# Two row units of the first token pass's down projection are added to the residual by one VectorE instruction

## Chip, cores and metric

The kernel runs on one core of a Trainium2 chip. The metric is the device time of one execution in microseconds (us), as the median of several runs. Engines are named as in the profile: PE is TensorE's matmul side, PEld its weight loads, DVE is VectorE, ACT is ScalarE, POOL is GpSimd, SP is the engine that issues most DMAs.

## The reference

The program is one step of a streaming encoder layer on 1152 tokens (1024 of a prompt, 8 x 16 of samples), with D = 1024 and a feed-forward width of 2816. After a convolution branch and an attention branch it computes:

```
def block_output(x, y_conv, y_attn, g_conv, g_attn, w_out, norm_ffn_w, w_gate, w_up, w_down):
    merged = jax.nn.sigmoid(g_conv) * y_conv + jax.nn.sigmoid(g_attn) * y_attn
    x = x + merged @ w_out
    xn = rms_norm(x, norm_ffn_w)
    return x + (jax.nn.silu(xn @ w_gate) * (xn @ w_up)) @ w_down
```

The change lies in the last line, in the sum of x and the product with w_down.

## The kernel before

All matrix products are done in fp32 accuracy with three passes of fp32r operands: high part by high part, low by high, high by low. So each weight block is split into a high part (by ACT, line 949) and a low part (by POOL, line 675). The split blocks go through a ring of 8 slots in SBUF.

The feed-forward part runs in two token passes. The first pass (p = 0) has token tiles 0, 2, 1, 3 of 128 tokens, the second (p = 1) has tiles 4, 6, 5, 7, 8. Within a pass the width 2816 is cut into 11 chunks of 256. For each chunk PE computes:

- a pair for w_gate (m = 0) and a pair for w_up (m = 1), each as seven products of a Strassen-Winograd scheme (line 1790, 12 matmuls each, into banks 0 to 3). DVE and ACT take the products out of PSUM as they come: ACT copies the first out as `prod` (line 1006), DVE makes the sums `u2`, `u3` and the gates (lines 1380 to 1417);
- then the down projection of the chunk before (function `down`, line 1851): for each half hf of the 1024 output columns, one row unit for each token tile. A row unit is six matmuls of 128x512 into one PSUM bank. In the first pass a down projection has 8 row units, numbered 0 to 7 in what follows (4 tiles for hf = 0, then 4 for hf = 1).

Row units of the down projection go round four banks, 4 to 7. PE may begin row unit n only when row unit n - 4 has been added to the residual X, because they share a bank:

```
if n >= 4:
    pe.wait_ge(y_free, n - 3)
```

`y_ready` counts row units that PE has finished, `y_free` those that DVE has added. `add_row` (line 1437) does one such addition, of 128x512 in PSUM to 128x512 of X in SBUF.

DVE works in program order. In chunk c, behind the pair for w_up, its order is: four `weight_sums` instructions (lines 1322 to 1327, sums of raw weight blocks for a later pair), the additions of row units 0 and 1, `h_lo_part` (line 1423, the low part of this chunk's activations, which waits for ACT), the additions of row units 2 to 7, four more `weight_sums`, and then line 1380 of the next pair. ACT's split of a summed block waits for the `weight_sums` instruction that makes it, and `prod` of the next pair stands behind such a split in ACT's order. PE's fifth product of a pair waits for `prod`, its sixth for the DVE's line 1390.

The last two chunks of the first pass are joined (the border, `border_down`) and keep their own order.

Of the kernel before, what the change touches and what calls it, by code (L numbers as in the profile page):

```python
# [28 lines left out]
ALU = mybir.AluOpType  # L29
# [50 lines left out]
PASS_TILES = ((0, 2, 1, 3), (4, 6, 5, 7, 8))  # L80
# [15 lines left out]
LAST_POS = {ht: n for n, ht in enumerate(LAST_ROWS)}  # L96
LAST_BASE = 6 * NT
# [3 lines left out]
def pair_unit(p, c, m):  # L101

    return 33 * p + (m if c == 0 else 3 * c - 1 + m)


def down_unit(p, c):

    return 33 * p + (4 + 3 * c if c < NCH - 1 else 32)
# [14 lines left out]
SLOT0, PROD0, ROW0 = [0], [0], [0]  # L123
# [9 lines left out]
def row_bank(n):  # L133

    return n % 4 + (0 if BORDER[0] <= n < BORDER[1] else 4)
# [25 lines left out]
def build(nc, io):  # L161
    ctx = ExitStack()
    with ctx:
# [3 lines left out]
        def sem(name):  # L167
            return ctx.enter_context(nc.semaphore(name))
# [87 lines left out]
        banks = ctx.enter_context(nc.psum_tensor("banks", [P, 8, 512], F32))  # L256
# [31 lines left out]
        d_ready, d_free = sem("d_ready"), sem("d_free")  # L288
# [7 lines left out]
        y_ready, y_free, border_used = sem("y_ready"), sem("y_free"), sem("border_used")  # L296
# [769 lines left out]
        def _(dve):  # L1066
# [5 lines left out]
            def norm_scale(ph, t):  # L1072

                xn, wbc = ((xn_p, wbc_p), (xn_f, wbc_f))[ph]
                pos = NORM_POS[t] if ph else t
                q = NT * ph + pos
                dve.wait_ge(sd_done, q + 1)
                dve.reciprocal(rms[:, t:t + 1], sd[:, t:t + 1]).then_inc(rms_done, 1)
                if ph == 0 and t >= 2:
                    dve.wait_ge(nT_done, 2 * (t - 1))  # L1080
                if ph == 1 and pos >= 2:
                    dve.wait_ge(tr_done, 2 * (pos - 1))
                dve.wait_ge(rms_done, q + 1)
                dve.scalar_tensor_tensor(out=xn[:, pos % 2, :], in0=X[:, t, :], scalar=rms[:, t:t + 1], in1=wbc[:, :],
                                         op0=ALU.mult, op1=ALU.mult).then_inc(xn_ready, 1)
# [227 lines left out]
            def weight_sums(r):  # L1313

                p, c, m = UNIT[r]
                q = pair_no(p, c, m)
                dve.wait_ge(f_raw[r % 2], 16 * RAW_PIECES * (r // 2 + 1))
                if r >= 3:
                    dve.wait_ge(f_lo, SLOT0[pair_unit(*divmod(q - 2, PAIRS)[:1], (q - 2) % PAIRS // 2, q % 2) + 1])
                elif r == 0:  # L1320
                    dve.wait_ge(d_ready, LAST_BASE)
                dve.tensor_tensor(w_sum(q, 0), raw_block(r, 1, 0), raw_block(r, 1, 1), ALU.add).then_inc(f_sum, 1)
                dve.wait_ge(f_sum, 4 * q + 1)
                dve.tensor_tensor(w_sum(q, 1), w_sum(q, 0), raw_block(r, 0, 0), ALU.subtract).then_inc(f_sum, 1)  # L1324
                dve.tensor_tensor(raw_block(r, 1, 0), raw_block(r, 0, 0), raw_block(r, 1, 0), ALU.subtract).then_inc(f_sum, 1)
                dve.wait_ge(f_sum, 4 * q + 2)
                dve.tensor_tensor(w_sum(q, 2), raw_block(r, 0, 1), w_sum(q, 1), ALU.subtract).then_inc(f_sum, 1)  # L1327

            def mix(i):

                def step(x, a, b):
                    dve.tensor_tensor(mix_cols(xc_f, i, x), a, b, ALU.subtract).then_inc(xc_T, 1)  # L1332

                dve.wait_ge(xc_copy, 3 * i + COPY_POS[B11])
                step(T1, mix_block(i, "B12"), mix_cols(xc_f, i, B11))
                dve.wait_ge(xc_copy, 3 * i + COPY_POS[B21 if i == 2 else B22])
                dve.wait_ge(xc_T, 4 * i + T_POS[T1])
                step(T2, mix_block(i, "B22"), mix_cols(xc_f, i, T1))
                dve.wait_ge(xc_copy, 3 * i + COPY_POS[B21])
                dve.wait_ge(xc_T, 4 * i + T_POS[T2])  # L1340
                step(T4, mix_block(i, "B21"), mix_cols(xc_f, i, T2))
                step(T3, mix_cols(xc_f, i, B22), mix_block(i, "B12"))

            def mix_lo(i, x):

                dve.wait_ge(xc_hi, 7 * i + HI_POS[x])
                dve.wait_ge(xc_T, 4 * i + 4)
                dve.tensor_tensor(mix_cols(xc[1], i, x), mix_cols(xc_f, i, x), mix_cols(xc[0], i, x).bitcast(F32),
                                  ALU.subtract).then_inc(xc_lo_dve, 1)

            def last_add(n):
                hf, t = LAST_ROWS[n]
                x = X[:, t, hf * 512:(hf + 1) * 512]
                dve.wait_ge(d_ready, LAST_BASE + n + 1)
                dve.wait_ge(d_free, NT * (4 + hf) + t + 1)
                dve.tensor_tensor(x, banks[:, 4 + n % 4, :], x, ALU.add).then_inc(d_free, 1)
# [62 lines left out]
            def h_lo_part(p, c):  # L1419
                ci, nb = NCH * p + c, HALF[p]  # L1420
                dve.wait_ge(h_hi, ci + 1)
                h = h_act[ci % 2]
                dve.tensor_tensor(h[:, 1, :, 0:2 * nb], Gt[ci % 2][:, :, 0:2 * nb], h[:, 0, :, 0:2 * nb].bitcast(F32),
                                  ALU.subtract).then_inc(h_lo, 1)

            def add_row(p, c, hf, k):
                tiles = PASS_TILES[p]
                t = tiles[k]
                n = ROW0[down_unit(p, c)] + len(tiles) * hf + k
                x = X[:, t, hf * 512:(hf + 1) * 512]  # L1430
                dve.wait_ge(y_ready, n + 1)
                if c == 0:
                    dve.wait_ge(d_free, LAST_BASE + LAST_POS[hf, t] + 1)
                else:
                    before = c - (2 if (p, c) == (0, NCH - 1) else 1)
                    dve.wait_ge(y_free, ROW0[down_unit(p, before)] + len(tiles) * hf + k + 1)
                dve.tensor_tensor(x, banks[:, row_bank(n), :], x, ALU.add).then_inc(y_free, 1)  # L1437

            def sums_ahead(r):
                if r + 2 < UNITS and UNIT[r + 2][2] < 2:  # L1440
                    weight_sums(r + 2)

            for p in range(2):
                last = NCH - 1
                for c in range(NCH):
                    border = p == 0 and c == last
                    pair(p, c, 0)
                    if (p, c) == (0, 0):
                        for n in range(14, len(LAST_ROWS)):
                            last_add(n)  # L1450
                    sums_ahead(pair_unit(p, c, 0))
                    if p == 0 and c in SCALE_AT:
                        norm_scale(1, SCALE_AT[c])
                    if p == 0 and c - TAIL_CHUNK in (1, 2):
                        for x in ((T2, T3), (T1, T4))[c - TAIL_CHUNK - 1]:
                            mix_lo(2, x)
                    if c == 1:
                        h_lo_part(p, 0)
                    pair(p, c, 1)
                    sums_ahead(pair_unit(p, c, 1))  # L1460
                    if border:
                        h_lo_part(p, c)
                        sums_ahead(down_unit(p, c - 1))
                        mix(3)
                        norm_scale(1, 7)
                        for k in range(len(PASS_TILES[p])):
                            add_row(p, c, 0, k)
                        for x in (T1, T4):
                            mix_lo(3, x)
                        mix(4)  # L1470
                        for k, x in enumerate((T2, T3, T1, T4)):
                            mix_lo(4, x)
                            add_row(p, c, 1, k)
                    elif c:
                        for hf in range(2):
                            for k in range(len(PASS_TILES[p])):
                                add_row(p, c - 1, hf, k)
                                if hf == 0 and k == 1:
                                    h_lo_part(p, c)
                        sums_ahead(down_unit(p, c - 1))  # L1480
                if p == 1:
                    for hf in range(2):
                        for k in range(len(PASS_TILES[p])):
                            add_row(p, last, hf, k)
                sums_ahead(down_unit(p, last))
# [435 lines left out]
```

## Time and profile before

| | |
|---|---|
| Median of 3 runs | 1702.14 us (1701.66 to 1703.0) |
| Profiled execution | 1702.15 us |
| Span of the profiled execution | 1700.4 us |
| PE busy | 1673.7 us (98%) |
| DVE busy | 959.4 us (56%) |
| POOL busy | 886.6 us (52%) |
| ACT busy | 694.9 us (41%) |

The span is the time from the first to the last instruction, and 1.75 us lie around it. Busy time of PE comes from matmuls whose ends are modelled, so the places where PE lost time are read from the starts of weight loads and from the lengths of the pieces in the chain that ended last.

### The profile page before, as it was taken

To read this page: it belongs to the slowest core of one execution; us is meant where nothing else is said; L and a number is where in the kernel's file an instruction comes from. 1 tells how busy PE (TensorE), PEld (TensorE's weight loads), DVE (VectorE), ACT (ScalarE), POOL (GpSimd) and SP (SyncE) were. 2 spreads that over 40 slices of the span, in tenths; PEclk is the share of its full clock that TensorE was granted. 3 is DMA by queue.
4 is the path that set the end of the run, shared out by engine and by line. 5 is a ranking of instruction groups with operands and counts; after the bars stand their busy time and mean duration, and the time that the engine had idled before them with its cause. 6 is when DMAs were issued, how large, how long until landed. Compare 5 with 4: busy or idle time off the path is not lost.

```text
span 1700.4 us, 27837 instructions
## 1 busy us (share of the span) xinstructions
PE 1673.7 (98%) x10510; PEld 1567.6 (92%) x10510; DVE 959.4 (56%) x1520; ACT 694.9 (41%) x1567; POOL 886.6 (52%) x808
## 2 busy tenths in 40 slices
PE   7999999999999999999999999999999999999999
PEld 7999888899889999999888899999989999999998
DVE  5466665636563412322568666757777555655555
ACT  6333566636665111111116444454454333333331
POOL 3544443333431212121239887887889656666662
PEclk9999999999999999999999999999999999999999
DMA  5211111111110111114121333233233222222222
GB/s 176 47 38 37 47 33 35 41 30 46 33 32 26 50 38 38 50 37 161 39 87 38 100 99 112 88 101 112 100 118 106 92 83 74 76 86 80 83 87 74
DMA packets 136057, 120.29 MB, mean 71 GB/s; under 512 B 24195, under 2 KB 117663, under 8 KB 135937
## 3 DMA queue, kind: packets, MB, share of 16 engines
q1 hardware_dynamic: 130400, 115.89, 21.7%
q10 hardware_dynamic: 4896, 2.36, 0.5%
q8 instruction: 76, 1.25, 0.3%
q0 software_dynamic: 640, 0.43, 0.1%
q14 instruction: 45, 0.36, 0.1%
HBM read 113.33 MB, written 5.32 MB: 70 GB/s over the span
## 4 chain that ended last, share of the span: by engine, by line
PE 94%; DVE 3%; issue 1%; ACT 1%; DMA 0%; SPq 0%; POOL 0%; DVEq 0%; ACTq 0%
PE banks L1504 37%; PE banks L1790 28%; PE banks L1851 15%; PE banks L1729 5%; PE banks L1667 2%; PE banks L1649 2%; PE banks L1527 1%; PE banks L1629 1%; PE banks L1540 1%; PE banks L1638 0%; DMA X<-in_x_prompt 0%; DVE w_sums L1327 0%; DVE xc_full L1332 0%; DVE w_sums L1324 0%; PE banks L1672 0%
## 5 line engine op out<-in xcount | busy, mean ns | idle before, releaser
L1504 PE MATMUL banks<-x_hi,w_hi 128*128 128x384 f32 x1200 | 410.7, 342 | 0.0
L1504 PE MATMUL banks<-x_hi,w_lo 128*128 128x384 f32 x1200 | 401.7, 335 | 0.0
L1504 PE MATMUL banks<-x_lo,w_hi 128*128 128x384 f32 x1200 | 401.6, 335 | 0.0
L1790 PE MATMUL banks<-xc_hi,ring_a 128*128 128x256 f32 (+1 forms) x1200 | 249.2, 298 | 3.9 <-DVE u L1399 3.9
L1504 PEld LDWEIGHTS banks<-x_hi,w_hi 128*128 128x128 f32 x1200 | 225.4, 188 | 4.4
L1504 PEld LDWEIGHTS banks<-x_lo,w_hi 128*128 128x128 f32 x1200 | 225.6, 188 | 0.0
L1504 PEld LDWEIGHTS banks<-x_hi,w_lo 128*128 128x128 f32 x1200 | 225.3, 188 | 0.0
L508 POOL TENSOR_TENSOR w_lo<-w_raw,w_hi 128x1024 fp32r<-128x1024 f32 x31 | 81.6, 2631 | 272.6 <-ACT w_hi L721 272.6
L1790 PEld LDWEIGHTS banks<-xc_hi,ring_a 128*128 128x128 f32 x1200 | 197.8, 191 | 4.5 <-DVE u L1399 4.1
L675 POOL TENSOR_TENSOR ring_a<-raw_f,ring_a 128x512 fp32r<-128x512 f32 x133 | 190.1, 1441 | 21.2 <-ACT ring_a L949 20.2
L516 POOL TENSOR_TENSOR w_lo<-w_raw,w_hi 128x256 fp32r<-128x256 f32 x84 | 60.7, 756 | 228.2 <-ACT w_hi L721 228.2
L1790 PE MATMUL banks<-xc_lo,ring_a 128*128 128x256 f32 (+1 forms) x600 | 178.3, 297 | 0.0
L1437 DVE TENSOR_TENSOR X<-banks,X 128x512 f32<-128x512 f32 x190 | 123.3, 684 | 36.6 <-PE banks L1851 36.6
L1790 PE MATMUL banks<-xc_hi,ring_o 128*128 128x256 f32 (+1 forms) x640 | 134.7, 296 | 0.0
L1851 PE MATMUL banks<-ring_a,h_act 128*128 128x512 f32 x570 | 132.5, 390 | 0.0
L1851 PEld LDWEIGHTS banks<-ring_a,h_act 128*128 128x128 f32 x570 | 106.1, 188 | 22.6 <-DVE X L1437 1.2
L675 POOL TENSOR_TENSOR ring_a<-w_sums,ring_a 128x512 fp32r<-128x512 f32 x63 | 88.1, 1398 | 74.4 <-ACT ring_a L949 74.4
L721 ACT ACTIVATE w_hi<-w_raw 128x1024 fp32r<-128x1024 f32 x60 | 63.5, 1058 | 151.8 <-PE banks L1504 89.8
L1790 PEld LDWEIGHTS banks<-xc_lo,ring_a 128*128 128x128 f32 x600 | 114.6, 191 | 0.4
L949 ACT ACTIVATE ring_a<-raw_f 128x512 fp32r<-128x512 f32 x133 | 81.8, 625 | 78.1 <-PE banks L1851 54.2
L1790 PEld LDWEIGHTS banks<-xc_hi,ring_o 128*128 128x128 f32 x640 | 105.7, 190 | 0.2
L1107 DVE RECIPROCAL branch<-branch 128x384 f32<-128x384 f32 x30 | 76.6, 2552 | 48.7 <-ACT branch L791 48.7
(229 smaller groups left out, 3414.3 us busy)
## 6 DMA issues: line engine op xcount, KB each, us to landing
w_raw<-in_w_in SPq DMA_DIRECT2D x104, 256.0 KB, 3.1
raw_f<-in_w_gate SPq DMA_DIRECT2D x88, 256.0 KB, 3.0
raw_f<-in_w_up SPq DMA_DIRECT2D x88, 256.0 KB, 3.2
raw_f<-in_w_down SPq DMA_DIRECT2D x88, 256.0 KB, 2.8
X<-in_x_prompt SPq DMA_DIRECT2D x16, 512.0 KB, 8.9
w_raw<-in_w_out SPq DMA_DIRECT2D x16, 256.0 KB, 3.0
out_y_prompt<-X SPq DMA_DIRECT2D x16, 256.0 KB, 2.0
X<-in_x_sample SPq DMA_DIRECT2D x2, 512.0 KB, 12.0
```

Of the source, the lines that this page charges most:

```text
L508: gp.tensor_tensor(ws[slab.slot][1][:, :], raw[slab.slot][:, :], ws[slab.slot][0][:, :].bitcast(F32), ALU.subtract).then_inc(w_lo, 1)
L516: ins = gp.tensor_tensor(ws[slab.slot][1][:, part], raw[slab.slot][:, part], ws[slab.slot][0][:, part].bitcast(F32), ALU.subtract)
L675: gp.tensor_tensor(slot_view(n, 1), slot_source(n), slot_view(n, 0).bitcast(F32), ALU.subtract).then_inc(f_lo, 1)
L721: act.activation(ws[slab.slot][0][:, :], raw[slab.slot][:, :], ACT.Copy).then_inc(w_hi, 1)
L949: act.activation(slot_view(n, 0), slot_source(n), ACT.Copy).then_inc(f_hi, 1)
L1107: dve.reciprocal(kr[:, bank[0], :], kr[:, bank[0], :]).then_inc(h_rs, 1)
L1437: dve.tensor_tensor(x, banks[:, row_bank(n), :], x, ALU.add).then_inc(y_free, 1)
L1504: mm = pe.matmul(banks[:, bank, 0:G], ws[slot][w][:, kt * P:(kt + 1) * P], xs[x][:, kt, g * G:(g + 1) * G], start=(kt == 0 and n == 0), st ...
L1649: mm = pe.transpose(banks[:, 5 + k, h * P:(h + 1) * P], Pb[:, (3 * t + u) % 2, h, k * P:(k + 1) * P], ident[:, :])
L1729: mm = pe.matmul(banks[:, bank, :], acts[act_slot][:, k, x, t * P:(t + 1) * P], ws[slot][w][:, k * 512:(k + 1) * 512], start=(k == 0 and n ...
L1790: mm = pe.matmul(banks[:, bank, 0:nb], ring(n)[:, w, k * P:(k + 1) * P], xc[x][:, X_OF_PROD[j], k, 0:nb], start=(start and k == 0 and z == 0),
L1851: mm = pe.matmul(banks[:, row_bank(n), :], rows, ring(SLOT0[r] + 2 * hf + k)[:, w, :], start=(k == 0 and o == 0), stop=(k == 1 and o == 2))
```

## The change

The first pass's additions for the down projections of chunks 0 to 8 are done two row units at a time. One DVE instruction reads two neighbouring PSUM banks (4 and 5, or 6 and 7) and adds them to two token tiles of X. It waits until both row units are there (`n + 2` where `add_row` has `n + 1`), and frees both banks together at its end. The border and the second pass keep `add_row`.

```diff
+            def add_two_rows(c, hf, k):
+
+                tiles = PASS_TILES[0]
+                n = ROW0[down_unit(0, c)] + 4 * hf + k
+                t, t2 = tiles[k], tiles[k + 1]
+                x = X[:, t:t2 + 1:t2 - t, hf * 512:(hf + 1) * 512]
+                dve.wait_ge(y_ready, n + 2)
+                if c == 0:
+                    dve.wait_ge(d_free, LAST_BASE + max(LAST_POS[hf, t], LAST_POS[hf, t2]) + 1)
+                else:
+                    dve.wait_ge(y_free, ROW0[down_unit(0, c - 1)] + 4 * hf + k + 2)
+                dve.tensor_tensor(x, banks[:, row_bank(n):row_bank(n) + 2, :], x, ALU.add).then_inc(y_free, 2)
+
...
+                    elif c and p == 0:
+                        for hf in range(2):
+                            for k in (0, 2):
+                                add_two_rows(c - 1, hf, k)
+                                if hf == 0 and k == 0:
+                                    h_lo_part(p, c)
+                        sums_ahead(down_unit(p, c - 1))
                     elif c:
                         for hf in range(2):
                             for k in range(len(PASS_TILES[p])):
```

On DVE this stands in the program behind the pair for w_up of each of the chunks 1 to 9. Shown is the first such place, with the lines of before behind a minus and those of the change behind a plus:

```order
 L1325 TENSOR_TENSOR raw_f<-raw_f 128x4x128
 L1327 TENSOR_TENSOR w_sums<-raw_f,w_sums 128x512
-L1437 TENSOR_TENSOR X<-banks,X 128x512 x2
+L1450 TENSOR_TENSOR X<-banks,X 128x2x512
 L1423 TENSOR_TENSOR h_act<-gate,h_act 128x2x512
-L1437 TENSOR_TENSOR X<-banks,X 128x512 x6
+L1450 TENSOR_TENSOR X<-banks,X 128x2x512 x3
 L1322 TENSOR_TENSOR w_sums<-raw_f 128x512
 L1324 TENSOR_TENSOR w_sums<-w_sums,raw_f 128x512
```

Eight additions become four of twice the size, one ahead of line 1423 and three behind it. Nothing else moves on DVE or on another engine.

## Rows read from the trace of the kernel before

**Rows 1.** The page, its total of busy time by engine.
```profile
PE 1673.7 (98%) x10510; PEld 1567.6 (92%) x10510; DVE 959.4 (56%) x1520; ACT 694.9 (41%) x1567; POOL 886.6 (52%) x808
```

**Rows 2.** Chain that ended last: start us, length us, engine, output, line, matmuls.
```profile
1121.62 10.91 PE banks L1851 x48
1132.53 20.27 PE banks L1790 x168
...
1163.71 20.15 PE banks L1790 x168
...
1324.67 13.74 PE banks L1851 x60
```

**Rows 3.** Waits of PE's weight loads: us in total, times, longest us.
```profile
PEld banks L1851 <- DVE X L1437: 2.2, 9, 0.3
```

**Rows 4.** Timeline of DVE: start us, length us, line, operation, operands, count, [idle before].
```profile
1125.00 1.28 DVE L1437 TENSOR_TENSOR X<-banks,X 128x512 f32<-128x512 f32 x2
1126.65 1.93 DVE L1423 TENSOR_TENSOR h_act<-gate,h_act 128x1024 fp32r<-128x1024 f32 x1 [0.37 <-ACT h_act L1036]
1128.51 2.47 DVE L1437 TENSOR_TENSOR X<-banks,X 128x512 f32<-128x512 f32 x4
...
1132.57 0.69 DVE L1437 TENSOR_TENSOR X<-banks,X 128x512 f32<-128x512 f32 x1 [0.67 <-PE banks L1851]
1133.18 1.59 DVE L1322 TENSOR_TENSOR w_sums<-raw_f 128x512 f32<-128x512 f32 x1
1134.80 1.67 DVE L1324 TENSOR_TENSOR w_sums<-w_sums,raw_f 128x512 f32<-128x512 f32 x1
```

**Rows 5.** Timeline of PEld, one short window each: first loads of row units 4, 6 and 7.
```profile
1126.71 0.19 PEld L1851 LDWEIGHTS banks<-ring_o,h_act 128*128 128x128 f32 x1
...
1129.43 0.19 PEld L1851 LDWEIGHTS banks<-ring_o,h_act 128*128 128x128 f32 x1
...
1130.79 0.19 PEld L1851 LDWEIGHTS banks<-ring_o,h_act 128*128 128x128 f32 x1
```

**Rows 6.** Groups of DVE by form: count | busy us, mean ns | idle us before.
```profile
L1437 DVE TENSOR_TENSOR X<-banks,X 128x512 f32<-128x512 f32 x190 | 123.3, 684 | 36.6 <-PE banks L1851 36.6
L1142 DVE COPY probsT<-banks 128x1024 f32<-128x1024 f32 x32 | 39.1, 1222 | 42.6 <-PE banks L1649 42.6
```

**Rows 7.** Timeline of DVE and PEld in the second pass, at its first row unit 6.
```profile
1331.94 1.27 DVE L1437 TENSOR_TENSOR X<-banks,X 128x512 f32<-128x512 f32 x2
1332.24 0.19 PEld L1851 LDWEIGHTS banks<-ring_a,h_act 128*128 128x128 f32 x1
1332.67 0.53 PEld L1851 LDWEIGHTS banks<-ring_a,h_act 128*128 128x128 f32 x3 [0.25 <-DVE X L1437]
```

**Rows 8.** Timeline of POOL behind the same down projection as Rows 4.
```profile
1132.91 1.31 POOL L675 TENSOR_TENSOR ring_a<-w_sums,ring_a 128x512 fp32r<-128x512 f32 x1
1134.16 1.76 POOL L675 TENSOR_TENSOR ring_o<-raw_f,ring_o 128x512 fp32r<-128x512 f32 x1
```

**Rows 9.** Timeline of ACT at the same place.
```profile
1136.58 0.64 ACT L949 ACTIVATE ring_o<-w_sums 128x512 fp32r<-128x512 f32 x1 [3.38 <-DVE w_sums L1324]
...
1137.64 0.37 ACT L1006 ACTIVATE prod<-banks 128x256 f32<-128x256 f32 x1
```

**Rows 10.** Timeline of PEld: starts of the fifth and sixth product of that pair.
```profile
1137.88 0.36 PEld L1790 LDWEIGHTS banks<-xc_hi,ring_a 128*128 128x128 f32 x2
...
1139.36 0.40 PEld L1790 LDWEIGHTS banks<-xc_hi,ring_a 128*128 128x128 f32 x2
```

**Rows 11.** Timeline of DVE, POOL and ACT behind the down projection of chunk 0.
```profile
976.20 0.69 DVE L1437 TENSOR_TENSOR X<-banks,X 128x512 f32<-128x512 f32 x1 [0.67 <-PE banks L1851]
...
977.72 1.67 DVE L1324 TENSOR_TENSOR w_sums<-w_sums,raw_f 128x512 f32<-128x512 f32 x1
...
977.09 1.76 POOL L675 TENSOR_TENSOR ring_a<-raw_f,ring_a 128x512 fp32r<-128x512 f32 x1
...
980.57 0.36 ACT L1006 ACTIVATE prod<-banks 128x256 f32<-128x256 f32 x1
```

## The prediction

> **What bounds the kernel.** I read the totals first: PE is busy 98% of the span, DVE 56% [rows 1]. So DVE's own time costs nothing by itself, and only what makes PE wait counts. Next the chain that ended last. In the first pass it alternates between two pieces of PE alone: 10.91 us for a down projection of 48 matmuls, and 20.15 or 20.27 us for the two pairs (168 matmuls) behind it [rows 2]. 10.91 / 48 is 0.227 us for a matmul, 1.36 us for a row unit, and the same for all nine down projections: PE waits nowhere in them. The pairs take 20.15 us behind six of the nine and 20.25 to 20.27 behind the down projections of chunks 3, 4 and 5: there PE loses 0.12 us. Last the waits: in the first pass PE's loads at line 1851 never wait for the additions. The 9 waits there are [rows 3] are in the second pass.
>
> So the question is how far ahead of PE each addition ends, and what follows the additions on DVE. I take the down projection of chunk 5 as the model. I compared the other eight: their starts relative to PE agree within 0.02 us up to row unit 7, and only the POOL instructions behind differ (below).
>
> **The durations.** One addition takes 0.684 us (128x512 from one bank) [rows 6]; back to back they start every 0.60 us (four in 2.47 us) [rows 4]. No DVE instruction of before adds two banks into X, so its price is bounded. Below: two starts at the pitch of 0.60, so 1.20 us, the new instruction then only dropping the gap. Above: two whole ones, 1.37 us. I take 1.22 us, since the COPY of 128x1024 out of two neighbouring banks takes 1.222 us [rows 6] and has the same elements per partition and the same two banks. The tiles of X lie two tiles apart, and I give that stride nothing, as one jump in 1024 elements. The Trainium skill has a formula for a fp32 `tensor_tensor` (VectorE: DVE Perf Modes, section on the TRN2 errata), (N + 151) / 0.96, which would make it 1224 ns; the 684 ns here against its 691 speak for it.
>
> **What is saved.** Each pair of additions occupies DVE for about 1.14 us (1.22 less the overlap of 0.08) where two took 1.20. 36 such pairs make 36 x 0.06 = 2.2 us of DVE time. By [rows 1] it is time of an engine that is idle for nearly half the span, so it shortens nothing on PE. Value in the sum: 0.
>
> **The cost at row unit 6.** PE may load for row unit 6 when row unit 2 has been added. Before, DVE comes to row unit 2 at 1128.51, behind line 1423, which ACT and then POOL hold up [rows 4]. The addition ends at 1128.51 + 0.68 = 1129.19. PE's first load of row unit 6 is at 1129.43 [rows 5], so it had 0.24 us to spare. Now the bank comes free when 2 and 3 are both added: 1128.51 + 1.22 = 1129.73. From the end of an addition to a load that waits for it goes 0.05 us: in the second pass the addition of 1331.94 ends at 1332.62 and the load is at 1332.67 [rows 7]. The load comes at 1129.78, 0.35 us late.
> How much of that does PE lose? The second pass shows it, as its row unit 6 is late now already: the load before is at 1332.24, the next was due 0.23 later, at 1332.47, and came at 1332.67, 0.21 us late [rows 7]. Its down projection takes 13.74 us for 60 matmuls [rows 2], against 60 x 0.227 = 13.64 without a wait, and in the starts of the matmuls that row unit is longer by 0.12. So 0.09 us of lateness is free, and the rest is lost. 0.35 - 0.09 = 0.26 us for each down projection, nine times.
>
> The other pairs are in time. Row unit 4 needs 0 and 1: they would end at 1125.00 + 1.22 = 1126.22, and the load is at 1126.71. Row unit 7 needs 3, which ends with 2, and its load at 1130.79 is a row unit later [rows 4, 5]. The addition of 4 and 5 ends before row unit 7 is finished.
>
> **The cost behind the down projection.** Before, row unit 7 alone was left: start 1132.57, `weight_sums` at 1133.18 [rows 4]. Now 6 and 7 wait for row unit 7 together: start 0.26 later with PE, 1.22 long, so line 1322 comes at 1133.97, 0.80 us later, of which 0.53 is lateness relative to PE. Behind it hang line 1324, ACT's split of its result (1136.58), another split, `prod` (1137.64) [rows 9], and PE's fifth product: two loads of 0.19 us span 0.36 us there, so the second comes 0.17 behind the first where 0.12 is the pitch of a pair (20.15 / 168), and 0.21 behind at the sixth (0.40) [rows 2, 10]. These are the 0.12 us above. So here lateness would be paid at once. But lines 1322 and 1324 do not run at their own 0.69: they take 1.59 and 1.67 us [rows 4], each ending about 0.57 after a POOL instruction does (1132.91 + 1.31 = 1134.22, then 1134.77) [rows 8]; POOL's next, 1.76 us, waits for DVE in turn. The two take turns. Two cases follow.
> - Chunks 3, 4, 5: DVE asks at 1133.97, still before POOL's end at 1134.22, and gets its turn as before. Line 1324 ends at the same time as before, while PE is 0.26 later. The 0.12 us that PE lost there is gone. Net 0.26 - 0.12 = 0.14.
> - The other six: POOL changes over at 977.09, DVE asks at 976.20 + 0.26 + 1.14 = 977.60 instead of 976.80, so POOL's next runs first and undisturbed, to about 978.4 (1.25 us). Line 1322 then ends at 978.98 and line 1324, with POOL idle, at 979.69 against 979.39 before (977.72 + 1.67) [rows 11]: 0.30 later, and PE is 0.26 later. `prod` begins 4.37 us behind row unit 7's addition here (980.57 - 976.20) and 5.07 in the first case, where it is just late, so some 0.65 us are free. Net 0.26.
>
> **The sum.** 6 x 0.26 + 3 x 0.14 = 2.0 us. Later stages start from PE's own signals and move with it; the border's waits begin with a DVE chain that PE starts. The profiled execution goes from 1702.15 to about 1704.1 us (span 1702.4), and since it equals the median of the runs, 1702.14, the forecast for the median is 1704.1, or 0.12% more. A measurement of this kernel can tell about 0.2%, 3.4 us, from no change, so this is "no change" with the sign of a loss.
>
> The Trainium skill weighs both ways in one section (Perfetto Trace Analysis, on optimizing Scalar and DVE operations). It says that larger operations help if the engine is saturated, and that where it isn't, but makes bubbles on others, instructions should be broken up. By the first, 36 times its 0.06 to 0.125 us of access overhead would be an estimated gain of 2 to 4.5 us; by the second a loss. The trace bears out the second, as DVE is at 56%.
>
> **Rivals.**
> - A. The lateness behind the down projection goes through. If DVE misses its turn in chunks 3 to 5 and line 1324 comes 0.53 us late relative to PE, PE pays 0.53 there and keeps the 0.12, in three chunks; the other six have 0.65 to spare. 9 x 0.26 + 3 x 0.53 = 4.0 us, 1706.1, slower by 0.23%. It decides once DVE asks after POOL's change at 1134.16, 0.19 us later than I work out. Against it: a POOL instruction that goes first (1.25 us) then leaves the next turn free. The rule behind it is in the Trainium skill (SBUF, who interferes with whom): with two SBUF inputs DVE blocks, and is blocked by, a GpSimd instruction for its whole length, in order of issue. The rows agree. Chance 0.14.
> - B. The instruction is dearer, up to 1.37 us: load 0.50 late, 0.41 lost, and DVE misses its turn in chunks 3 to 5 at no gain: 9 x 0.41 = 3.7 us, 1705.9. Chance 0.07.
> - C. Row unit 6 isn't late, since line 1423 gets its turn before POOL's in the new order (it waits 0.8 us of its 1.93 [rows 4]), so additions begin that much earlier. Then no loss at line 1851, and the 0.12 may go or stay: 1701.8 to 1702.2. Against it: everything ahead of 1126.65 is as before, relative to PE. Chance 0.13.
> - D. DVE's saved 2.2 us reaches PE: 1700. Only if DVE bound these chunks, which [rows 2] denies. Chance 0.02. A gain over 0.2% would need 3.4 us, more than all of it.
> - The forecast: 0.64.
>
> **Range.** From C, 1702.0, to a little above A, 1706.3; C's lowest and a sum of A and B (about 1707) are left out, near 2 in 10 with what noise does. The likeliest case alone spans 1703.3 to 1704.9. Slower by over 0.2% (above 1705.5): A, B in part, 0.17. Faster: 0.02. Within: 0.81.
>
> **What the profile after should show.** The new line 36 times at 1.22 us. PEld at line 1851 waiting for it 9 times, about 0.38 us each (0.35 and the usual gap of 0.04). Down projections of 11.17 us where 10.91 stood, and pairs of 20.15 everywhere. Line 1322 shorter than 1.59 behind chunks 3 to 5. The second pass unchanged. I would be wrong if the pieces of the pairs grew beyond 20.3, if the new instruction took over 1.3 us, or if line 1851 showed no wait.

## The result, and the profile after

| | before | with the change |
|---|---|---|
| Median | 1702.22 us (1701.57 to 1704.45, 20 runs) | 1705.41 us (1704.16 to 1707.13, 20 runs) |
| Ratio | | 1.0018 (95% interval 1.0012 to 1.0024) |
| Span of the profiled execution | 1700.4 us | 1703.5 us |

The change makes the kernel slower by 0.18%, 2.0 to 4.1 us by the interval. The forecast was 1704.1 us, 1.9 above this median of before, in a range of 1702.0 to 1706.3. With 20 runs of each kernel the interval is 0.06% to either side, so a loss of 0.18% stands clear of zero; the 0.2% that the prediction took as the least to be told from no change was too much.

First the page of the changed kernel, its total by engine.

```profile
PE 1675.1 (98%) x10510; PEld 1565.9 (92%) x10510; DVE 952.1 (56%) x1484; ACT 692.8 (41%) x1567; POOL 883.5 (52%) x808
```

DVE has 36 instructions fewer and is busy 7.3 us less [rows 1]. The additions account for 2.3 us of that (123.3 before [rows 6], 77.1 + 43.9 now). Most of the rest is in `weight_sums`, whose wait for a turn counts as busy: line 1324 took 5.9 us less in all, line 1322 1.4 us more (both cases are below). None of it reaches the end of the program.

The groups of DVE by form: the new line stands beside what is left of line 1437 (border and second pass).

```profile
L1437 DVE TENSOR_TENSOR X<-banks,X 128x512 f32<-128x512 f32 x118 | 77.1, 684 | 28.6 <-PE banks L1871 28.5
L1450 DVE TENSOR_TENSOR X<-banks,X 128x1024 f32<-128x1024 f32 x36 | 43.9, 1219 | 17.6 <-PE banks L1871 15.9 <-issue 1.7
```

One double addition takes 1.219 us, where 1.22 was taken from a copy of the same size [rows 6]. Line 1871 is the old 1851, and 1810 the old 1790.

The chain that ended last, in the places that answer to [rows 2]:

```profile
1103.53 20.15 PE banks L1810 x168
1123.69 11.17 PE banks L1871 x48
1134.86 20.15 PE banks L1810 x168
1155.01 11.17 PE banks L1871 x48
...
1327.74 13.75 PE banks L1871 x60
```

Of the nine down projections of the first pass seven are longer by 0.26 us (10.91 before) and two, those of chunks 0 and 2, by 0.29. The pairs behind chunks 3 to 5 are shorter by 0.10 to 0.12 (20.25 to 20.27 before). The second pass is as it was.

The waits of PE's weight loads, which answer to [rows 3]:

```profile
PEld banks L1871 <- DVE X L1450: 3.4, 9, 0.4
PEld banks L1871 <- DVE X L1437: 2.2, 9, 0.2
```

Nine new waits of 0.38 us, one for each down projection, beside the nine in the second pass.

And one of them, in the timelines of DVE and of PEld behind chunk 6's pairs (compare [rows 4, 5]; this profile is 2.06 us later at the first load of this down projection):

```profile
1128.71 1.93 DVE L1423 TENSOR_TENSOR h_act<-gate,h_act 128x1024 fp32r<-128x1024 f32 x1 [0.44 <-ACT h_act L1036]
1130.56 1.21 DVE L1450 TENSOR_TENSOR X<-banks,X 128x1024 f32<-128x1024 f32 x1
1131.96 1.23 DVE L1450 TENSOR_TENSOR X<-banks,X 128x1024 f32<-128x1024 f32 x1 [0.19 <-issue]
1134.95 1.23 DVE L1450 TENSOR_TENSOR X<-banks,X 128x1024 f32<-128x1024 f32 x1 [1.76 <-PE banks L1871]
1136.09 0.71 DVE L1322 TENSOR_TENSOR w_sums<-raw_f 128x512 f32<-128x512 f32 x1
1136.84 1.66 DVE L1324 TENSOR_TENSOR w_sums<-w_sums,raw_f 128x512 f32<-128x512 f32 x1
...
1131.83 1.22 PEld L1871 LDWEIGHTS banks<-ring_o,h_act 128*128 128x128 f32 x6 [0.38 <-DVE X L1450]
```

The addition of row units 2 and 3 ends at 1130.56 + 1.21 = 1131.77, and PE's load for row unit 6 stands ready and goes at 1131.83. Line 1322 takes 0.71 us here, not 1.59 [rows 4], and line 1324 ends at 1138.50, which is 0.03 us earlier than before once the 2.06 us are taken off.

Behind the down projection of chunk 0, the prediction's second case, DVE and POOL show (compare [rows 11]; this profile is 0.91 us later here):

```profile
978.59 1.36 DVE L1322 TENSOR_TENSOR w_sums<-raw_f 128x512 f32<-128x512 f32 x1
979.99 0.69 DVE L1324 TENSOR_TENSOR w_sums<-w_sums,raw_f 128x512 f32<-128x512 f32 x1
...
978.11 1.30 POOL L675 TENSOR_TENSOR ring_a<-raw_f,ring_a 128x512 fp32r<-128x512 f32 x1
```

POOL's instruction runs first and undisturbed in 1.30 us where it took 1.76, line 1322 ends behind it, and line 1324 runs in its own 0.69 us and ends at 980.68, or 979.77 without the 0.91; 979.69 was forecast.

### The profile page after: what moved, and what is told of

It reads as the page before. It is cut to its first block, busy times and chain, and to the rows that moved or that the text cites. A ratio compares the mean times of both kernels' runs of the same rounds, so it can differ in the third digit from the quotient of the medians.

```text
span 1703.5 us, 27765 instructions
## 1 busy us (share of the span) xinstructions
PE 1675.1 (98%) x10510; PEld 1565.9 (92%) x10510; DVE 952.1 (56%) x1484; ACT 692.8 (41%) x1567; POOL 883.5 (52%) x808
## 4 chain that ended last, share of the span: by engine, by line
PE 94%; DVE 4%; issue 1%; ACT 1%; DMA 0%; SPq 0%; POOL 0%; DVEq 0%; ACTq 0%
PE banks L1524 37%; PE banks L1810 28%; PE banks L1871 15%; PE banks L1749 5%; PE banks L1687 2%; PE banks L1669 2%; PE banks L1547 1%; PE banks L1649 1%; PE banks L1560 1%; DVE xc_full L1332 1%; PE banks L1658 0%; DMA X<-in_x_prompt 0%; DVE w_sums L1327 0%; DVE w_sums L1324 0%; DVE w_sums L1322 0%
## 5 line engine op out<-in xcount | busy, mean ns | idle before, releaser
L675 POOL TENSOR_TENSOR ring_o<-raw_f,ring_o 128x512 fp32r<-128x512 f32 x66 | 94.1, 1434 | 9.4 <-ACT ring_o L949 9.0
```

The costliest lines, as they stand in the source:

```text
L675: gp.tensor_tensor(slot_view(n, 1), slot_source(n), slot_view(n, 0).bitcast(F32), ALU.subtract).then_inc(f_lo, 1)
```

## The experiments

The kernels were measured in three series, e1 to e4, e5 to e8 and e9 to e12 (the expectations say "call"), each beside the kernel before. The table has for each kernel the difference in us of its median to that of before in the same series, and the length of one stretch of its profile: from the first load of the first down projection to the first load of the second pass's first down projection. Every instruction that the change touches lies in it. Before, it is 359.39 us long, in the two controls 359.23 and 359.28. The down projection is the time from its first load to the next pair's first, the median of nine; it is about 0.1 us less than the piece in the chain (10.80 for 10.91). The ratio is worked out from all runs and is not the quotient of the two medians, so where both are noise (e5) their signs can differ.

```
                                median   ratio (interval)          stretch  down proj.  row 6 load gap
change                           +3.2    1.0018 (1.0012, 1.0024)    361.56    11.06       0.57
e1 change again                  +2.7    1.0016 (1.0007, 1.0025)    361.56    11.06       0.57
e2 only 2,3 doubled              +3.0    1.0016 (1.0007, 1.0025)    361.16    11.05       0.57
e3 all doubled but 2,3           +0.9    1.0006 (0.9997, 1.0015)    359.55    10.80       0.23
e4 all doubled, line 1423 later  +1.0    1.0005 (0.9996, 1.0014)    359.58    10.80       0.23
e5 before, as control            -0.1    1.0002 (0.9993, 1.0011)    359.23    10.80       0.23
e6 small delay                   -0.5    1.0000 (0.9991, 1.0009)    359.34    10.80       0.23
e7 large delay                   +4.4    1.0028 (1.0017, 1.0038)    363.45    11.31       0.83
e8 singles, line 1423 later      +0.0    1.0000 (0.9991, 1.0009)    359.28    10.80       0.23
e9 before, as control            -0.5    0.9999 (0.9989, 1.0008)    359.28    10.80       0.23
e10 change, third time           +1.9    1.0015 (1.0006, 1.0024)    361.57    11.06       0.57
e11 e3 again                     -0.5    1.0000 (0.9991, 1.0009)    359.59    10.80       0.23
e12 four by one instruction     +30.7    1.0173 (1.0159, 1.0188)    389.60    13.62       0.23
```

The gap is from the last load of row unit 5 to the first of row unit 6, normally 0.23 us.

### The change again (e1, e10)

> The changed kernel once more, as a scale for the others. Its profile showed 2.16 us more than before between the first down projection and the second pass, while the medians are 3.2 us apart. Theory R (only the bank that row unit 6 waits for costs time): the stretch again grows by 2.1 to 2.2 us, and the medians lie 2.0 to 2.7 us apart. Rival L (something outside that stretch belongs to the changed program as well): the medians are again about 3.2 us apart, and the profile shows about 1 us more than before in front of the first down projection, at the same place as last time (around 197 us).

> The changed kernel in the same call as the second control. The stretch again 2.1 to 2.2 us longer. Theory N: median 1.8 to 2.7 us above before. Rival L: 2.7 to 3.3 us.

Both came out in the stretch to 0.01 us: 361.56 and 361.57, 2.2 us longer than before. The medians were 2.7 and 1.9 us above before, at the edge of theory R and inside theory N. The extra time around 197 us, which rival L asked for, is not in the profile of e1 but is in that of e10. More on this in the part on the controls.

### Which of the four double additions costs (e2, e3)

Shown is the edit of e2; in e3 the condition is `!=`.

```diff
-                                add_two_rows(c - 1, hf, k)
+                                if (hf, k) == (0, 2):
+                                    add_two_rows(c - 1, hf, k)
+                                else:
+                                    add_row(p, c - 1, hf, k)
+                                    add_row(p, c - 1, hf, k + 1)
```

> Only row units 2 and 3 are added by one instruction (9 instructions), the other six singly. Theory R: the loss is all here. PE's load for row unit 6 waits 9 times, down projections of 11.17 us, pairs of 20.15, and the same time as the whole change within 0.5 us. Rival S (the late end of the additions behind row unit 7 is what costs): row unit 7 is added alone, so most of the loss goes and the time is within 0.7 us of before.

> Row units 0 and 1, 4 and 5, 6 and 7 are added in pairs, 2 and 3 singly (27 double instructions, 18 single). Theory R: no load at the down projections waits, they take 10.91 us, the pairs behind chunks 3 to 5 keep their 20.27, and the time is that of before within 0.5 us. Rival S: line 1322 starts 0.5 us later relative to PE, so pairs of about 20.8 behind chunks 3 to 5 (1.6 us in all) and a time 1 to 2 us above before.

The waits of the loads, first of e2, then of e3 (line 1875 is the old 1851):

```profile
PEld banks L1875 <- DVE X L1450: 3.4, 9, 0.4
PEld banks L1875 <- DVE X L1437: 2.2, 9, 0.2
```

```profile
PEld banks L1875 <- DVE X L1437: 2.2, 9, 0.3
```

With 2 and 3 alone doubled, all nine waits are there, and the down projection is as long as with the whole change. With the three other pairs doubled and 2 and 3 single there is none in the first pass; the nine that are left are those of the second. In e3 the late end behind row unit 7 is still there, as DVE and the chain of e3 show:

```profile
1133.12 1.23 DVE L1450 TENSOR_TENSOR X<-banks,X 128x1024 f32<-128x1024 f32 x1 [1.50 <-PE banks L1875]
1134.26 0.96 DVE L1322 TENSOR_TENSOR w_sums<-raw_f 128x512 f32<-128x512 f32 x1
1135.26 1.67 DVE L1324 TENSOR_TENSOR w_sums<-w_sums,raw_f 128x512 f32<-128x512 f32 x1
```

```profile
1122.12 10.91 PE banks L1875 x48
1133.03 20.23 PE banks L1814 x168
```

Line 1322 comes later here, but takes 0.96 us instead of 1.59: what it came late it had been spending on the wait for POOL. Counted from the first load of the next pair, line 1322 starts at 1.62 us instead of 1.03, and line 1324 ends at 4.29 instead of 4.32. The pair is 20.23 us long, not the 20.8 of the rival. So the late start behind row unit 7 costs nothing in the pairs, which is the rival refuted.

A small part of the stretch does hang on it, at the border. From the first load behind the ninth down projection to the first of the second pass it takes 98.87 to 98.91 us in the three profiles of before, 98.99 to 99.02 in the three of the change, 99.18 in e3 and 98.72 in e2, where row unit 7 is added alone. In 13 of the 14 profiles this is 95.26 to 95.32 us more than the time at which line 1324 ends there, counted from the same load (3.62 before, 3.70 with the change, 3.88 in e3, 3.41 in e2); only e12 differs. So a later end of line 1324 seems to be passed on there in full; the path from one to the other was not followed. It is the 0.2 to 0.3 us by which the stretch of e3 is longer than before, and most of the 0.4 by which that of e2 is shorter than the change's. The median of e3 was 0.9 us above before, outside the 0.5 of theory R; e11, the same program, came out 0.5 us below before.

### Row units 2 and 3 added ahead of line 1423 (e4, e8)

```diff
-                                if hf == 0 and k == 0:
+                                if hf == 0 and k == 2:
                                     h_lo_part(p, c)
```

In e8 the same is done to the kernel before: in the first pass `h_lo_part` stands behind row unit 3 instead of 1.

> All four double additions as in the change, but line 1423 (h_lo_part) stands behind the addition of 2 and 3 instead of ahead of it. Theory R: 2 and 3 are added as soon as row unit 3 is there, about 5.7 us behind the first load of the down projection, and end 1 us before row unit 6 needs the bank. No wait at row unit 6, down projections of 10.91 us, and the time is that of before or up to 0.4 us less. Rival S: what comes behind row unit 7 is not changed by this, so the loss of the whole change stays.

> Single additions as before, with line 1423 behind the addition of row unit 3 in the first pass, ahead of 4. Theory R: before, the addition of row unit 2 was 0.24 us early and cost nothing, so moving it further ahead gains nothing: down projections of 10.91 us, the pairs behind chunks 3 to 5 still about 20.3, the same time as before within 0.5 us. A theory by which these waits already cost something in the kernel before: up to 1 us less.

The timeline of DVE in e4, around the first two double additions behind chunk 6's pairs:

```profile
1124.67 1.22 DVE L1450 TENSOR_TENSOR X<-banks,X 128x1024 f32<-128x1024 f32 x1
1126.86 1.23 DVE L1450 TENSOR_TENSOR X<-banks,X 128x1024 f32<-128x1024 f32 x1 [0.97 <-issue]
1128.01 1.51 DVE L1423 TENSOR_TENSOR h_act<-gate,h_act 128x1024 fp32r<-128x1024 f32 x1
```

All four double additions remain, 2 and 3 end at 1128.09, 1.0 us before PE's load for row unit 6 at 1129.10, and the loss at the down projections is gone: 10.91 us in the chain, and a stretch of 359.58, 0.2 to 0.3 us above before by the border. The median was 1.0 us above before where theory R had it level or up to 0.4 us less; the part on the controls comes back to that. The place of row units 2 and 3 behind line 1423 and their joint release are both needed for the loss. Singles moved in the same way (e8) gain nothing, since nothing waited there.

### Lateness without a double read (e6, e7)

The kernel before, with one or two copies out of row unit 2's bank ahead of its addition; nothing reads what they write. Shown is the edit of e7; e6 has one copy, into `u2_f`, of the first 64 columns.

```diff
+                                if p == 0 and (hf, k) == (0, 2):
+                                    n = ROW0[down_unit(p, c - 1)] + 2
+                                    dve.wait_ge(y_ready, n + 1)
+                                    for out in (u2_f, u3_f):
+                                        dve.tensor_copy(out[:, 0:320], banks[:, row_bank(n), 0:320])
                                 add_row(p, c - 1, hf, k)
```

> The kernel before with single additions, and ahead of the addition of row unit 2, nine times in the first pass, one copy of 128x64 out of its bank into u2, which nothing reads. The copy costs about 0.13 us of DVE at this place. Theory R: the addition of row unit 2 had 0.24 us to spare, less 0.05 for the signal, so no load waits, down projections stay at 10.91 us and the time is that of before. A theory by which any further DVE work at this place costs: 9 x 0.13 = 1.2 us more.

> As the small delay, with two copies of 128x320 (into u2 and u3, which nothing reads there), about 0.80 us of DVE in all. Theory R: the load for row unit 6 comes 0.80 + 0.05 - 0.24 = 0.61 us late, of which 0.09 are free: 0.52 lost in each of nine down projections (11.43 us), 0.36 given back in the pairs, 4.3 us in all. Rival (the loss of the change belongs to reading two banks with one instruction): no instruction here reads two banks, so no loss.

The timeline of DVE in e6, the chain in e7 (line 1856 is the old 1851), and e7's waits:

```profile
1127.91 0.21 DVE L1481 COPY u<-banks 128x64 f32<-128x64 f32 x1
1128.05 3.25 DVE L1437 TENSOR_TENSOR X<-banks,X 128x512 f32<-128x512 f32 x5
```

```profile
1131.63 0.47 DVE u L1481
1132.10 0.61 DVE X L1437
1132.71 0.04 issue
1132.76 3.01 PE banks L1856 x12
1135.77 20.15 PE banks L1795 x168
```

```profile
PEld banks L1856 <- DVE X L1437: 8.0, 18, 0.6
```

The small delay of 0.14 us fits in what was spare (0.24 less the 0.05 of the signal): no wait, no loss. The large one makes the load 0.60 us late and each down projection 0.51 us longer, with single additions throughout. The chain now leads from PE to the copies, to the addition and back to PE. The stretch grew by 4.1 us, 4.3 were forecast. So a late release of the bank is enough for the loss, and a read of two banks is not needed for it; e3 and e4 show that such a read alone brings none.

### Four row units by one instruction (e12)

```diff
+                dve.wait_ge(y_ready, n + 4)
...
+                x = X[:, 0:4, hf * 512:(hf + 1) * 512].rearrange("p (b a) c -> p a b c", a=2)
+                y = banks[:, 4:8, :].rearrange("p (a b) c -> p a b c", a=2)
+                dve.tensor_tensor(x, y, x, ALU.add).then_inc(y_free, 4)
```

> Four row units of one half are added by one instruction over banks 4 to 7, in the place of two and two; line 1423 stands behind the first. Theory R (the loss is the lateness of the bank that the next row unit waits for, less 0.09 us): row unit 3 is there 5.67 us behind the first load, the instruction takes 2.29 us (1.22 + 2 x 0.533), so the load of row unit 4 comes at 8.01 instead of 5.37, 2.64 late, 2.55 lost, nine times, less 0.36 in the pairs: 22.6 us more than before, down projections of 13.45 us. Row units 5 to 7 wait for nothing. Rival S (a later end behind row unit 7 costs): the end is 1.6 us later relative to PE, of which 0.65 are free, and pairs grow from 20.15 to about 21, 8 us on top of that.

The group of the instruction, and the chain over one down projection (line 1882):

```profile
L1462 DVE TENSOR_TENSOR X<-banks,X 128x2048 f32<-128x2048 f32 x18 | 41.2, 2292 | 64.5 <-issue 64.5
```

```profile
1142.30 3.46 PE banks L1882 x16
1145.75 2.10 issue
1147.86 2.30 DVE X L1462
1150.29 5.72 PE banks L1882 x24
1156.02 20.15 PE banks L1821 x168
```

The instruction takes the 2.29 us that were worked out, and the pairs stay at 20.15. The piece of 2.10 us called "issue" is no pause of PE: DVE waits there for row unit 3, and PE works on until that is done and then stands still while the instruction runs, as its timeline shows:

```profile
1144.65 3.11 PE L1882 MATMUL banks<-ring_a,h_act 128*128 128x512 f32 x13
1150.29 0.93 PE L1882 MATMUL banks<-ring_o,h_act 128*128 128x512 f32 x3 [2.53 <-DVE X L1462]
```

The second rival is refuted here too, by the same way as in e3: line 1322 starts 1.66 us later than before, counted from the next pair's first load (2.69 against 1.03), but takes 0.68 us, and line 1324 ends at 4.10 us, earlier than the 4.32 before behind chunks 3 to 5. What a clearly later end of line 1324 would cost the pairs, no run tests. The load of row unit 4 comes 8.25 us behind the first instead of 5.37 (I had 8.01: row unit 3's last matmul has to run out first). That is 2.88 late, and in the five down projections at full clock PE loses 13.61 - 10.80 = 2.81. The other four are 1.4 to 1.6 us longer still; this is the granted clock, below. So the stretch grew by 30.2 us where 22.6 were forecast: 9 x 0.26 us from the later load, and 5.9 us from the clock, are what the forecast lacked, less 0.6 us that the border is shorter here (98.24). The table of waits names POOL for these loads, not DVE:

```profile
PEld banks L1882 <- POOL ring_a L675: 11.7, 4, 2.9
PEld banks L1882 <- POOL ring_s L675: 8.8, 3, 2.9
PEld banks L1882 <- POOL ring_o L675: 5.8, 2, 2.9
```

These nine waits of 2.9 us are those for the additions. The load waits for the split weights and for the bank, and one of the two is named; the chain has the right one: DVE ends at 1150.15 and the load goes at 1150.26, while POOL's last instruction ahead of it ended at 1149.39.

### The controls (e5, e9, e11)

> The kernel before, run as if it were a changed one. The runs so far have medians some 0.7 to 1 us above what their stretch between the first down projection and the second pass explains (0.2 us more in the stretch, 0.9 us more in the median, for two of them). Theory N (this rest belongs to the comparison or to chance, not to the change): this control too comes out 0.5 to 1 us away from its own twin, or within 0.3 us and the rest stays within the intervals. Rival L (the rest belongs to the changed programs): this control agrees with its twin within 0.3 us, while the other kernels of this call stand 0.7 to 1 us above what their stretch explains.

> Second control: the kernel before against itself, in one call with two kernels of the first call. Open is a rest: for the changed kernel and for those with double additions the median stands 0.5 to 1.2 us further above before than the stretch from the first down projection to the second pass explains, in the second call the rest was -0.5 to 0.4 us. Theory N (chance of the call): with all in one call, the rests of the control and of the other two lie within 0.5 us of each other. Rival L (the rest belongs to programs with the new function): the control's rest is near 0, theirs 0.5 to 1.2 us.

> All additions doubled but 2 and 3, again. The stretch within 0.2 us of before. Theory N: median within 0.5 us of before. Rival L: 0.7 to 1 us above it, as in the first call.

Subtract from each median the growth of its stretch. What is left is +1.0 us for the change, +0.5, +1.2, +0.8, +0.8 for e1 to e4, between -0.5 and +0.4 for e5 to e8, and -0.4, -0.3, -0.7 for e9, e10, e11. (For e12 it is +0.5, from five runs of 1727 to 1735 us, of which the profile is the longest.) In the last series the kernel before and two with the new function lie together, as theory N had it, and e3 has gone from +0.9 to -0.5 with its stretch unchanged (359.55, 359.59). So most of what is left goes with the series and not with the program.

A part of it does belong to the program. A run's time is longer than its span, and by how much hardly varies: by 1.69 to 1.81 us in every run of before in the three series and of e2, e3, e5 to e9, e11 and e12, but by 2.03 to 2.15 us in every run of the change, e1, e10 and e4. That is 0.34 us more, outside the span, for the two programs that add all pairs of the nine down projections by the double instruction. No run shows the cause. For these two programs the rival that the changed program costs something elsewhere is right by 0.34 us, a third of the 1.0 us that was open. With it taken off, the rests of the change are +0.7, +0.2 and -0.6 (e1 and e10 the last two), and that of e4 is +0.5.

Another part can be seen in the profiles of before and after. In stretches 196 to 200 us (busy us and instructions of PE, PEld, DVE, ACT and POOL, then PE's granted clock as a share of 2.4 GHz, DMA share and GB/s), first before, then after:

```profile
196.00:200.00 4.00, 4.00 (x36) 3.83 (x35) 3.93 (x5) 2.09 (x5) 3.85 (x7) 1.00 0.75 219
```

```profile
196.00:200.00 4.00, 4.00 (x21) 3.77 (x20) 3.96 (x3) 1.99 (x5) 3.49 (x6) 0.62 0.79 231
```

In the changed kernel's profile the granted clock was at 1.2 GHz for 3.4 us around here, and PE did 21 matmuls instead of 36; the comparison of starts before and behind this place gives 1.6 us. This is in the attention stage, which runs the same instructions in both. Of the 1.6 us some 0.65 are made up elsewhere, and 0.9 us are left between the profiles ahead of the first down projection (964.97 and 965.88 us). Such pieces come and go: both profiles have one near 941 us, and before has one near 913. The one near 197 us is in the profiles of the change, e2, e10 and e12, not in that of e1, which is the same program, nor in those of e3, e4 and e11, and in none of the six without the new function. So the program alone does not decide it; whether it comes more often with the new function, 14 profiles are too few to say.

## Why the prediction was right

- **What bounds.** Right: PE's own chain, into which one wait for a bank came. The prediction counts 20.15 us behind six down projections. It is so behind chunks 0, 2, 6 and 7; behind chunk 1 eight matmuls of another line lie between the two pairs, and behind chunk 8 the border follows. Neither changed, so the sum does not depend on it.
- **The instruction.** 1.22 us taken, 1.219 measured; the stride over X cost nothing.
- **What is saved.** DVE's busy time fell and PE's chain took nothing of it. The section of the Trainium skill cited in the prediction (Perfetto Trace Analysis, on optimizing Scalar and DVE operations) holds here by its second half: with DVE at 56%, larger instructions made bubbles, the nine waits of 0.38 us.
- **Row unit 6.** Forecast a load 0.35 late and 0.26 lost, nine times. Measured: gap 0.57, so 0.34 late, and 11.06 - 10.80 = 0.26 lost. The waits 9 and 0.38 each, as forecast. The rule that the first 0.09 us are free came from the second pass (0.21 late, 0.12 lost [rows 7]); with e7 (0.60 late, 0.51 lost) and e12 (2.88, 2.81) it holds within 0.02 at all four.
- **Behind the down projection.** Both cases as forecast: line 1322 got its turn ahead of POOL in chunks 3 to 5 (it came 1136.09 - 1133.18 = 2.91 us later than before, 0.85 without the 2.06 by which this down projection begins later; forecast 0.80), and those pairs fell to 20.15. Behind chunk 0, as the model of the other six, line 1322 began at 978.59 - 0.91 = 977.68 (forecast 977.60) and line 1324 ended at 979.77 (forecast 979.69), and those pairs stayed as they were. Rival A, that DVE misses its turn in chunks 3 to 5 and the lateness goes through, is ruled out by the rows of the change, and by e3 with single 2 and 3.
- **The sum.** 2.0 forecast; the stretch is 361.56 to 361.57 us in three profiles against 359.23 to 359.39 in three of before, 2.2 to 2.3 more. Against the profile of before the 2.17 us are 2.42 at the nine down projections (2.34 forecast), 0.34 given back in the pairs (0.36 forecast), and 0.08 at the border, where line 1324 ends 0.08 us later and which the sum had at nothing.
- **The median.** 1704.1 forecast, 1705.41 measured. That is above the 1703.3 to 1704.9 of the likeliest case alone and nearer to the times of rivals A and B (1706.1 and 1705.9); by the median alone they could not be told apart, and it is the rows that decide. Above the 2.17 us of the stretch stand 1.0 us: 0.34 outside the span, which the sum lacked, and the rest by chance of the runs. The repeats were 2.7 and 1.9 above before. The mean of the three is 2.6 us, against 2.17 + 0.34 = 2.5, and all three intervals hold 2.2 as well as 2.5 us.
- **Rival B** (dearer instruction), **C** (row unit 6 not late) and **D** (saved time reaches PE) are ruled out by the rows above: 1.219 us, nine waits, no gain. (Redone, A's sum is 3.9 us and B's time 1705.8; nothing hangs on either.)

## What to carry to other kernels

When one instruction empties several PSUM banks, all of them come free at its end. Look for the bank that the producer needs next and how early it was free before: here it had 0.24 us to spare, and joining its addition with the next put the release 0.54 us later (1.22 against 0.68). Joining costs almost nothing where the additions are far ahead of the producer (e3, or e4 after a small reorder: 0.2 to 0.3 us of stretch, at the border). It gained nothing here in any form; whether it pays where the consuming engine is the bound, no run here shows. And a later start of an instruction that waits for a turn anyway is not a later end: what it hangs behind has to be in the sum.

## What the runs showed that was not expected

- How late a load may be: of the lateness of a load at a row unit PE loses all but 0.07 to 0.09 us (four points from 0.21 to 2.88 us late; none is below 0.09, so that such a load would cost nothing is inferred). The rows of loads show how it is made up: behind the late load the next follows after 0.108 us instead of 0.227 (the change, e2, the second pass; 0.109 in e7), so that 0.12 us is caught up at once, of which the loads behind it give some 0.04 back.
- The stretch is the same within 0.16 us in three profiles of the kernel before and within 0.01 us in three of the change, while medians of 11 to 20 runs differ by a microsecond from series to series. For changes this small the stretch tells more than the median, but it can't see what lies outside it: the 0.34 us between span and time are in no profile.
- With PE standing still for 2.5 us in each down projection (e12), the granted clock fell to half, 1.2 GHz, for 3.4 us in four of the nine, 1.4 to 1.6 us of loss each. With the waits of 0.38 us of the change there was no such piece in the stretch in any of three profiles.
